# Gates of two dense blocks added in DRAM by index, and three blocks spread, in a hybrid gMLP / short-conv / PEER layer

## The reference

```
q = (xb @ w_q).reshape(t, 8, 2, 128)
s = einsum('thpd,hpkd->thpk', q, sub_keys)           # 128 keys on each of two sides
s1, i1 = top_k(s[:, :, 0], 16); s2, i2 = top_k(s[:, :, 1], 16)
top_s, sel = top_k(all 16 x 16 sums, 16); idx = i1 * 128 + i2 of the chosen
gate = softmax(top_s)                                # 8 heads x 16 experts per token
act = gelu(einsum('thkd,td->thk', expert_u[idx], xb))
ffn = einsum('thk,thkd->td', gate * act, expert_v[idx])
```

## Time and profile before

| | |
|---|---|
| median of 3 runs | 2945.51 us |
| single runs | 2946.67, 2930.32, 2945.51 us |
| span of the profiled execution, first to last instruction | 2939.3 us |
| TensorE busy | 2830.0 us, 96% |
| VectorE busy | 2512.5 us, 85% |
| ScalarE busy | 885.5 us, 30% |
| GpSimd busy | 1029.0 us, 35% |
| data moved | 917.54 MB, 312 GB/s on average |
| mean granted clock of TensorE | 0.990 |

### The profile page before, as it was taken

The page is one execution under the profiler, slowest core; times in us unless marked ns, Lnnn a source line. Parts: engine busy times, 40 slices in busy tenths (PEclk is TensorE's granted clock), DMA queues, the critical chain, the costliest instruction groups (busy, mean ns, idle before and its releaser), DMA issues. The chain is left out here.

```text
span 2939.3 us, 47358 instructions
## 1 busy us (share of the span) xinstructions
PE 2830.0 (96%) x19184; PEld 1834.9 (62%) x19184; DVE 2512.5 (85%) x4708; ACT 885.5 (30%) x1321; POOL 1029.0 (35%) x778
## 2 busy tenths in 40 slices
PE   4999999998999999999999999999999999999998
PEld 4566686766667877677776677777544444444443
DVE  6876556987887879999999999998699999999877
ACT  3333532221111432222222344444222222222223
POOL 0000000002776025444554532222456566655410
PEclk9999999999999999999999999999999999999999
DMA  8989653433999458888888999999999999999972
GB/s 328 348 318 381 238 199 129 144 123 115 391 392 378 192 215 288 303 325 314 330 315 320 354 327 346 350 346 341 368 398 405 405 388 414 407 401 404 364 267 115
DMA packets 222971, 917.54 MB, mean 312 GB/s; under 512 B 20208, under 2 KB 61216, under 8 KB 181536
## 3 DMA queue, kind: packets, MB, share of 16 engines
q1 hardware_dynamic: 61664, 427.91, 37.3%
q0 software_dynamic: 110592, 402.70, 36.4%
q10 hardware_dynamic: 50496, 83.89, 7.9%
HBM read 771.79 MB, written 142.63 MB: 311 GB/s over the span
## 5 line engine op out<-in xcount | busy, mean ns | idle before, releaser
L1718 PE MATMUL psU<-hB,w 128*128 128x320 f16 (+2 forms) x3104 | 927.4, 299 | 27.4 <-ACT Z L753 15.9
L1719 PE MATMUL psU<-hB,w 128*128 128x320 f16 (+2 forms) x3104 | 927.3, 299 | 0.0
L1720 PE MATMUL psU<-hB,w 128*128 128x320 f16 (+2 forms) x3104 | 927.0, 299 | 0.0
L753 ACT ACTIVATE w<-stage 128x2048 f16<-128x2048 f32 x176 | 335.7, 1909 | 606.1 <-PE psX L1720 331.2
L1043 DVE SCALAR_TENSOR_TENSOR w<-stage,w 128x2048 f16<-128x2048 f32 x176 | 402.3, 2287 | 99.4 <-ACT w L753 99.4
L746 POOL DMA_INDIRECT rows<-in_u_rows,idx_sp x200 | 267.8, 1339 | 376.0 <-DVE rows L1139 233.5
L1718 PEld LDWEIGHTS psU<-hB,w 128*128 128x128 f16 x3104 | 304.9, 98 | 140.2 <-issue 22.9
L1720 PEld LDWEIGHTS psU<-hB,w 128*128 128x128 f16 x3104 | 305.1, 98 | 117.6
L1719 PEld LDWEIGHTS psU<-hB,w 128*128 128x128 f16 x3104 | 305.0, 98 | 110.4
L746 POOL DMA_INDIRECT rows<-in_v_rows,idx_sp x205 | 271.4, 1324 | 285.4 <-DVE rows L1139 184.5
L1718 PE MATMUL psX<-w,Z 128*128 128x512 f16 x768 | 292.2, 381 | 7.6 <-DVE Z L1641 4.2
(11 more groups left out here) (263 smaller groups left out, 4435.8 us busy)
## 6 DMA issues: line engine op xcount, KB each, us to landing
stage<-in_u_units SPq DMA_DIRECT2D x64, 1024.0 KB, 8.8
stage<-in_v_units SPq DMA_DIRECT2D x64, 1024.0 KB, 8.0
stage<-in_w_front SPq DMA_DIRECT2D x48, 1024.0 KB, 8.6
hl_dram<-w SPq DMA_DIRECT2D x48, 1024.0 KB, 6.5
w<-hl_dram SPq DMA_DIRECT2D x48, 1024.0 KB, 7.2
a_dram<-R ACTq DMA_DIRECT2D x64, 640.0 KB, 8.0
g_dram<-Z ACTq DMA_DIRECT2D x20, 2048.0 KB, 10.7
Z<-a_dram SPq DMA_DIRECT2D x32, 1280.0 KB, 11.8
```

Of the source, the lines that this page charges most:

```text
L753: return nc.scalar.activation(dst, src, func, scale=scale)
L1718: mm(ps, lhs[0](k), rhs[0](k), start=start and s == 0, stop=False)
L1719: mm(ps, lhs[0](k), rhs[1](k), start=False, stop=False)
L1720: last = mm(ps, lhs[1](k), rhs[0](k), start=False, stop=stop and s == n - 1)
```

## The change

Of the five dense blocks only the first three (DV = 3, NV = 384 tokens) are still spread, in 12 units from E48 on (N_SPREAD 20 to 12, E_SPREAD 40 to 48). For the last two (DS = 2, TS = 256 tokens) the gates are **added in DRAM by index**: a second array `gs_dram`, 16384 x 256 float32 (16.8 MB), is zeroed by 16 stores of 1 MB that ScalarE's queue issues after units 42 to 57 of the list (the time of V2, V3 of set B and the Q units of set A), and GpSimd issues 2 x 8 x 16 = 256 indirect DMAs that each add one gate for each of 128 tokens. They are issued one before each row gather in E8 to E47, two before each in E48 to E57, until all are out; the pairs for a head wait for that head's gates. Ranks keep their place (E0 to E35). The softmax is now made head by head: the subtraction of head h by VectorE in unit 5h+1 behind the ranking pieces, the exponential by ScalarE at the end of unit 5h+2, the division and the addresses by VectorE in unit 5h+3; for the last head in E36, E37 and E38. `_sections` keeps its rule with the new E_SPREAD, so that slots come as 2 and 3 in turn up to E43. `product` takes four instructions of 384 columns from the spread gates and one of 4 x 256 from the others, which a second load per pair of groups brings.

```diff
+DS = 2
+DV = DB - DS
+NV = DV * P
+TS = DS * P
...
-N_SPREAD = NT // 32
+N_SPREAD = NV // 32
 E_SPREAD = 2 * NGRP - N_SPREAD - 4
+E_RANK = 36
+ZERO_FIRST, ZERO_N = N_OF["B", "V", 2], 16
+HEAD_SHIFT = {min(5 * h + 1, E_RANK): h for h in range(HEADS)}
+HEAD_EXP = {min(5 * h + 2, E_RANK + 1): h for h in range(HEADS)}
+N_SCATTER = DS * HEADS * TOPK
+SCATTER_FIRST, SCATTER_LAST = 8, 2 * NGRP - 6
...
+                    sp.dma_start(G_s[pair % 2].rearrange("p h j t -> p (h j) t"), gs_dram[pair]
+                                 ).then_inc(g_in[pair % 2], 16)
...
+            for b in range(DS):
+                sp.wait_ge(gs_added[b], 16 * HEADS * TOPK)
...
+            def add_gates(n):
+                for _ in range(min(n, N_SCATTER - added[0])):
+                    h, b, k = added[0] // (DS * TOPK), added[0] // TOPK % DS, added[0] % TOPK
+                    if b == 0 and k == 0:
+                        pool.wait_ge(scatter_ready, h + 1)
+                    if h and k == 0:
+                        pool.wait_ge(gs_added[b], 16 * TOPK * h)
+                    i = b * P + h * TOPK + k
+                    pool.indirect_dma_start(gs_flat, bass.IndirectOffsetOnAxis(ap=at_s[:, i:i + 1], axis=0),
+                                            gate_s[:, i:i + 1], None, compute_op=ALU.add).then_inc(gs_added[b], 16)
+                    added[0] += 1
+            pool.wait_ge(gs_zeroed, 16 * ZERO_N)
+            for m, (table, slot, c) in enumerate(ROWS):
+                _, kind, u = SEC_UNITS[c]
+                if kind == "E" and SCATTER_FIRST <= u < SCATTER_LAST:
+                    add_gates(1 if u < E_SPREAD else 2)
...
+                if ZERO_FIRST <= n < ZERO_FIRST + ZERO_N:
+                    part = gs_zero[n - ZERO_FIRST]
+                    act.dma_start(part, zeros.unsqueeze(1).to_broadcast([P, part.shape[1], D])).then_inc(gs_zeroed, 16)
...
-                if (x, kind, u) == ("B", "E", E_SPREAD - 4):
-                    act.wait_ge(s_shift, 2)
-                    activation(s_all["B"], s_all["B"], ACT.Exp).then_inc(s_exp, 1)
+                if kind == "E" and u in HEAD_EXP:
+                    h = HEAD_EXP[u]
+                    act.wait_ge(s_shift, 2 + h)
+                    activation(s_all["B"][:, :, h, :], s_all["B"][:, :, h, :], ACT.Exp).then_inc(s_exp, 1)
...
+            def shift_head(h):
+                step(V.tensor_copy(most, s3[:, :, 0:1]))
+                settle()
+                V.tensor_tensor(s3, s3, most.to_broadcast([P, DB, TOPK]), ALU.subtract).then_inc(s_shift, 1)
+            def gates_head(h):
+                for b in range(DS):
+                    step(V.tensor_scalar(i1, i1, float(TS), tok[:, b:b + 1], ALU.mult, ALU.add))
+                    settle()
+                    step(V.scalar_tensor_tensor(i2, i2, float(P * TS), i1, ALU.mult, ALU.add))
+                settle()
+                step(V.tensor_copy(at, i2_all["B"][:, DV:DB, h, :]))
+                dve.wait_ge(s_exp, 2 + h)
+                step(V.tensor_reduce(total, s3, AX_X, ALU.add))
+                settle()
+                step(V.reciprocal(inv, total))
+                settle()
+                V.tensor_tensor(s3, s3, inv.unsqueeze(2).to_broadcast([P, DB, TOPK]), ALU.mult).then_inc(gate_ready, 1)
+                dve.wait_ge(gate_ready, 2 + h)
+                settle()
+                V.memset(unread[:, :], 0.0).then_inc(scatter_ready, 1)
...
+                    a = A_t[g % 2][:, j, 0:NV].rearrange("p (n t) -> p n t", t=32)
+                    step(V.scalar_tensor_tensor(a, a, AS, G_t[g // 2 % 2][:, :, g % 2, j, :], ALU.mult, ALU.mult))
+                a = A_t[g % 2][:, :, NV:NT]
+                ins = V.scalar_tensor_tensor(a, a, AS, G_s[g // 2 % 2][:, g % 2], ALU.mult, ALU.mult)
...
-                if kind == "E" and u == E_SPREAD - 5:
+                if kind == "E" and u == E_RANK - 1:
                     rank_some("B", 7, 9)
-                    shift_scores("B")
-                if kind == "E" and u == E_SPREAD - 3:
-                    gates("B", 2)
+                if kind == "E" and u in HEAD_SHIFT:
+                    shift_head(HEAD_SHIFT[u])
+                if kind == "E" and u - 1 in HEAD_EXP:
+                    gates_head(HEAD_EXP[u - 1])
```

More of the change, by code:

```diff
@@ L175 @@
 X_IDX = X_QB + HEADS * QT["B"]
-X_G = X_IDX + 6
-X_END = X_G + NT // 4
+X_G = X_IDX + 3
+X_END = X_G + NV // 4
 def _h_set(x, first_x, first_h, shift, split):
@@ L489, in trunk_layer @@
         row_in = [sem(f"row_in{i}") for i in range(18)]
+        zeros_ready = sem("zeros_ready")
+        gs_zeroed = sem("gs_zeroed")
+        gs_added = [sem(f"gs_added{b}") for b in range(DS)]
+        scatter_ready = sem("scatter_ready")
         end_in = sem("end_in")
@@ L721, in _ @@
             pool.iota(iota_i[:, :], pattern=[[1, P]], base=0, channel_multiplier=0).then_inc(ident_ready, 1)
+            pool.iota(tok_i[:, :], pattern=[[P, DS]], base=0, channel_multiplier=1).then_inc(ident_ready, 1)
+            pool.memset(zeros, 0.0).then_inc(zeros_ready, 1)
+            pool.wait_ge(zeros_ready, 1)
             for i in range(2):
@@ L729, in _ @@
             pool.memset(acc_sp[:, :, :], 0.0).then_inc(acc_zeroed, 1)
-            for m, (table, slot, _) in enumerate(ROWS):
+            added = [0]
+            def add_gates(n):
[14 more added lines that the diff above has]
+                    add_gates(1 if u < E_SPREAD else 2)
                 r, before, _ = PLACES[m]
@@ L828, in indices_out @@
             def indices_out(lo, hi):
[L830 to L833, removed]
+                for kind in range(lo, hi):
+                    a = X_IDX + kind
                     wait_x(act, a)
                     if kind < 2:
-                        pairs = slice(first * P // 2, last * P // 2)
-                        activation(keys_t16[:, pairs, kind, :], psX[a % 4][:, 0:n].rearrange("p (n t) -> p n t", t=2)
+                        activation(keys_t16[:, :, kind, :], psX[a % 4][:, 0:NV].rearrange("p (n t) -> p n t", t=2)
                                    ).then_inc(x_free[a % 4], 1)
                     else:
-                        activation(g_t[:, at], psX[a % 4][:, 0:n], ACT.Copy, GS).then_inc(x_free[a % 4], 1)
+                        activation(g_t, psX[a % 4][:, 0:NV], ACT.Copy, GS).then_inc(x_free[a % 4], 1)
             def section_gelu(n):
@@ L1480, in idx_t @@
             def idx_t():
-                for i in range(4):
-                    a = X_IDX + 5 - i
+                for a in range(X_IDX, X_G):
                     dve.wait_ge(x_free[a % 4], a // 4 + 1)
@@ L1596, in _ @@
                     rank_some("B", 0, 9)
-                elif kind == "E" and u < E_SPREAD - 4:
+                elif kind == "E" and u < E_RANK:
                     h = min(1 + (u - 1) // 5, 7)
@@ L1851, in index_tiles @@
                 for i in range(lo, hi):
-                    flat = (i1_all, i2_all, s_all)[i // 2]["B"].rearrange("p b h k -> p b (h k)")
-                    first, last = SPLIT["B"][i % 2]
+                    flat = (i1_all, i2_all, s_all)[i]["B"].rearrange("p b h k -> p b (h k)")
                     ps = x_tile(X_IDX + i)
-                    for b in range(first, last):
-                        ins = nc.tensor.transpose(ps[:, (b - first) * P:(b - first + 1) * P], flat[:, b, :], ident[:, :])
+                    for b in range(DV):
+                        ins = nc.tensor.transpose(ps[:, b * P:(b + 1) * P], flat[:, b, :], ident[:, :])
                     ins.then_inc(x_ready, 1)
```

54 lines of the change are left out of this document (34 added, 20 removed).

## The result

The changed kernel takes 3174.19 us (median of 6 executions, 3164.36 to 3184.35) against 2945.6 of the kernel before beside it: a ratio of 1.0808, 95% interval 1.0773 to 1.0842.

What follows compares the result with a forecast made beforehand. Ranking: TensorE and VectorE both near their limit; spread units: VectorE; W: TensorE. Terms -33.0 - 0.6 + 16 + 3 + 1.5 + 17 = +3.9 us, applied to the median 2945.51, gave 2950 us, range 2905 to 3045.

Steps and rivals of the forecast that it cites:

- Item 1: Eight spread units become plain ones, 17.1 to 12.97 us each: -33.0 us, and -0.6 for casts and transposes.
- E32's stall: Ranking, kernel before: TensorE stood 6.3 us at one unit, psU tiles having run out; forecast to go.
- Item 2: Gates per head: ScalarE's wait for VectorE's subtraction stalls TensorE, 11 us at head 0; +16 us (0 to +35).
- rival A: Everything is covered: VectorE's small work fits its gaps, ScalarE's waits stay under 10 us; 2912 us, chance 0.20.
- Item 3: 256 indirect adds on GpSimd, priced like row gathers at 1.24 us start to start: +3, +1.5 and +17 us.
- It fits, barely: Ranking: one cycle's rows and adds ask 78.4 of 80.6 us of GpSimd.
- C: An add is dearer on GpSimd than a gather, 1.76 us start to start: about 3040 us, chance 0.22.
- D: Both sides' reads of an add generated one after the other, 2.18 us: about 3147 us, chance 0.08.
- The spread units: First 7.5 spread units: 12 GpSimd instructions each ask 16.4 or 17.4 against 17.1 us; +1.5 us (0 to +8).
- Rows later by order: E8 to E35: rows behind adds on GpSimd come later, 0.6 us a unit in 28 units; +17 us (0 to +40).
- Item 4: Small parts: zero stores hidden, the product's fifth instruction 0, gates in 1 KB pieces 0 (-2 to +15).
- The stretch beside VectorE: GpSimd instructions meeting VectorE's line 1043 are held: about 1.5 us per unit charged; without it about -20 us.

Runs made afterwards that it cites:

- E8: Not a run: unit number 8 of kind E, in the ranking; its end is placed by ScalarE's store, at 1198.88 us before the change and 1197.49 after.
- E47: Not a run: unit number 47 of kind E, spread before the change and plain after it; its end is placed by ScalarE's store.
- E0: Not a run: unit number 0 of kind E, where the ranking begins; its end is placed by ScalarE's store.
- E35: Not a run: unit number 35 of kind E, in the ranking; its end is placed by ScalarE's store.
- no_adds: The changed kernel without its 256 indirect adds, so the gates of the two last blocks are missing: 2932.75 us, ratio 0.994.
- E39: Not a run: unit number 39 of kind E, the last before the kernel before began spreading; its end is placed by ScalarE's store.
- E29: Not a run: unit number 29 of kind E, in the ranking; its end is placed by ScalarE's store.
- E30: Not a run: unit number 30 of kind E, in the ranking; its end is placed by ScalarE's store.
- plain_write: The changed kernel with its scatters overwriting instead of adding: 3077.56 us, ratio 1.0401.
- half_adds: The changed kernel with every second add left out, the others in their places: 2977.09 us, ratio 1.0083.
- half_grouped: half_adds with the same adds issued in groups, once per unit, ahead of the row GpSimd has to wait for anyway: 2960.68 us, ratio 1.0069.

## Why the prediction was wrong, point by point

**Item 1, the spread units**, held: -33.6 forecast. no_adds goes from E39 to E47 in 105.3 us, before it was 145.1: -39.8, of which E32's stall is no part; the twelve left, with the entry into spreading now among them, took 211.0 there for 205.3. Together that is -34.1.

**Item 2, the heads**, was over-priced at +16; its mechanism appeared once. ScalarE's timeline at E2:

```profile
1112.41 0.27 ACT L803 ACTIVATE Z<-Z 128x80 f32<-128x80 f32 x1 [17.63 <-DVE Z L1532]
...
1114.10 1.40 ACT L803 ACTIVATE R<-psU 128x320 f32<-128x320 f32 x4
```

I had said 15 to 20 us of waiting and 11 of stall; TensorE stood 10.4 us. Yet from the store of E0 to that of E8 it took 125.6 us, before 125.0. In no_adds the waits for the subtraction were 17.37, 3.14 and 1.98 us at the first three heads, so the 5 and 4 us of heads 1 and 5 never came, E32's stall went, and TensorE had no gap in E8 to E47. From the store of E0 to that of E39, ahead of all spread units, no_adds takes 607.5 us and the kernel before 611.8: the net is -4, below my lower bound of 0. Without adds the time is that of rival A but for W: 2933 measured, 2912 + 21.5 for the pieces, and 2915 with long ones. Its condition failed, ScalarE's wait of 17.4 us at head 0 being over its 10, and that the sum meets the time to 1 us is luck: against the kernel before as it ran beside no_adds (2950.7) the gain is 18 us and not 12.

**Item 3, the adds**, is the step that failed: "the nearest rows are the row gathers with as many indices: 0.94 us and 0.30 to the next, 1.24 start to start". An add takes 1.80 + 0.30 = 2.10, even the shortest 1.56 + 0.30, and a plain scatter with the same indices 1.25 in the mean. "It fits, barely" went with that price: from E8 to E47 GpSimd was asked for 167 us more than the stretch has. I had weighed 1.76 (C) and 2.18 (D) as rivals and named 1.35 as the point from which the price decides, but gave both together 0.30. The arithmetic behind D was sound: it has +84 for E8 to E29 where E8 to E30 lost 78.8, and +88 for E30 to E47 where no_adds to after is +80.7. Its reason, two reads generated one after the other, fits the 1.59 against 0.98 in direction only (it would be 1.88); no run tested it.

A second error lies in the forecast's own figure. Even at the gather's price the adds were to cost 3 + 1.5 + 17 us; plain_write lost 145 against no_adds. The 0.94 I took is a floor, while the rows that I quoted under the earlier trace rows had means of 1.31 and 1.15. With the 1.5 us a unit for line 1043 my sum had 78.4 / 56 = 1.40 from start to start over rows and adds. Measured are 1.28 + 0.30 for 227 rows and 1.25 + 0.30 for 188 writes: 650 us, 64 over by E47 (54 by the window, in which 219 rows fall), and the fixed order adds 37.

**The spread units** lost 84.5 us against no_adds where D had 51. Eight adds and four rows per unit ask 8 x 2.1 + 4 x 1.5 = 22.8 of 17.1 us, 43 in seven and a half units. The first of the twelve, with the entry, took 57.1 us against 23.0; in it TensorE once waited 37.8 us for the first one-hots.

**Rows later by order, +17** for E8 to E35: a real effect, 23 us by half_adds against half_grouped, by the mechanism that I had described.

**Item 4**, "the same bytes of gates come in 1 KB pieces ...: 0 (-2 to +15)": 21.5 us, just outside the bound. I had the warning, a DMA share of 1.01 in that stage, and priced bytes where pieces count. The zeros cost nothing that these runs show: the store of E0 came at 1071.9, before at 1073.9, and in all runs with zeros at 1071.8 to 1084.7, so some us can't be told.

**The stretch beside VectorE.** I charged 1.5 us a unit, for line 1043 alone. The traces bear the mechanism out and have more of it. That product is line 1096 in the changed kernel; the add below is the one of 1411.19 above.

```profile
1410.02 2.29 DVE L1096 SCALAR_TENSOR_TENSOR w<-stage,w 128x2048 f16<-128x2048 f32 x1
```

The product ends at 1412.31 and the add at 1413.77, 1.46 later. All 17 adds of the changed kernel that begin over 0.05 us into this product end 1.43 to 1.48 us behind it, and all 52 such gathers of the kernel before end 0.81 or 0.82 behind it, whether they last 1.89 or 3.04 us. Of the 369 gathers there that begin over 0.1 us into a dot product (L1139) or a weighted sum (L1148) none ends sooner than 0.81 us behind it either, and the 82 inside L1503 end 0.81 or 0.82 behind it; these I had not charged. The gather quoted in the earlier trace rows began 0.03 us before its product and was held all the same; of those that began 0.1 to 0.3 us before it none was. The Trainium skill's page SBUF - State Buffer, section on what grabs the shared port pair, has products of two tensors leave descriptor generation alone. The traces disagree, and they decide: L1043, L1139 and L1503 each read two tensors. No run took these products away; it is the fixed end times that show the hold.

## What to carry to other kernels

Before an operation goes onto an engine with "35% busy", add up that engine's occupancy in each stage, with mean durations and the gap behind each instruction, and compare it with the stage's length: here 227 us were free where 395 were asked. If the operation has no row in the trace, ask from what price on the answer changes sign; where that lies only 9% above the row taken (1.35 to 1.24), the outcome is open and the chances should say so. Put such fill-in work where the engine waits anyway, not one before each urgent item, and lay out data that is loaded later in long pieces.

## What the runs showed of the hardware that was not expected

- An indirect add of 128 values of 4 bytes holds GpSimd for at least 1.56 us and 1.80 in the mean; the same as a plain scatter 0.97 and 1.25, as a gather of 4 bytes 0.94 and 1.15. The price hangs on the accumulation, not on the bytes: row gathers of 4 KB have the same floor of 0.93 to 0.94.
- Loading 1 MB in pieces of 1 KB landed in 26.6 to 28.1 us in the W stage, the same megabyte in pieces of 8 KB in 19.4 to 19.7, and that was worth 21.5 us of the whole.
- The adds are 36864 packets of the software queue (147456 in place of 110592), 144 per instruction, the plain scatters 8192, 32 per instruction (118784 in plain_write's page). The row gathers beside them did not land later for it (medians of 5.4 to 6.1 us from issue to landing in 1200 to 1940; before, 7.8 to 9.3 in 1200 to 1686, with more transfers beside them).
- A gather that GpSimd begins over 0.05 us into VectorE's product of line 1043 ends 0.81 or 0.82 us behind that product (52 of 52, before), an add 1.43 to 1.48 (17 of 17, after), whenever in it they began.
